# Input projections of a hybrid decoder step on one core: order of weight splits, bias table, key turns and bias strips

## The chip, the cores and the metric

The kernel runs on one core of a Trainium2 chip. The metric is the device time of one execution in microseconds (us); lower is better. Before the change the median of three runs is 2732.77 us (2732.03 to 2739.77).

## The reference

The reference is one inference step of two layers, for a prompt of 1024 tokens and 8 samples of 8 tokens each (64 rows). The change touches the first stage of layer 0:

```python
def attn_projections(xn, w_in, ...):
    h = jnp.einsum('btd,de->bte', xn, w_in)          # xn = rmsnorm(x), 1024 wide
    qa, ka, va, qi, ki, wi, hb = jnp.split(h, ...)
    q_a = rmsnorm(qa per head); k_a = rmsnorm(ka per head)
    ...                                              # three window groups: q_b, k_b normed, v_b
sc   = sum over 8 heads of wi * relu(qi . ki)        # index scores, then top 256 keys of each row
bias = rel_bias[rel_bucket(distance)]                # one table of 32 buckets x 20 heads
```

Sparse attention, window attention, the output projection, the squared-ReLU MLP and a recurrent layer with its own MLP follow in later stages.

## The kernel before, in words

The whole kernel is written by hand for five engines with semaphores. `stage_project` (line 363) is the first stage. It multiplies 9 tiles of rows (tile 0 holds the 64 sample rows, tiles 1 to 8 the prompt, 128 rows each) with 8 groups of columns, `GROUPS`: group 0 `kikv` (328 columns: index keys, index weights, keys, values), group 1 `qi` (index queries, 512), group 2 `qa`, groups 3 to 5 `qk0..2`, group 6 `v01`, all 512, and group 7 `v2` (256). Below, "(g, i)" is tile i of group g, and a step is one such pair.

A product is made in three passes of fp32r with a high and a low part of both operands: (x high, w high), (x high, w low), (x low, w high), for each of 8 slices k of the contraction, so 24 matmuls a tile (`project`, line 772; its `piece` and `pieces` cut the 24 into equal runs). Group 0's first seven tiles run slice by slice as the input arrives (line 846).

The weights of a slice k of a group, a "unit", come in by DMA from SyncE's queue (`load_w`, line 515) into one of three raw buffers. VectorE makes the high part (`split_high`, line 922), GpSimd the low part (`split_unit_low`, line 600). A raw buffer is free for the unit three later when its low part is made. A group may begin on TensorE when all 8 low parts of it are there (`w_low`).

ScalarE copies a finished tile out of PSUM into one of three row buffers (line 721, `copied`), squares the heads that have a norm (line 741), and takes the roots one step later (line 674). VectorE sums the squares (`norm_sum`), inverts the roots of the tile before and multiplies (`norm_apply`, line 975). GpSimd multiplies by the gains (line 640, `gained`), and SyncE stores the row buffer (`store`, line 533). ScalarE may overwrite a row buffer when it is stored. A tile p on TensorE needs the rows of tile p-3 copied, since there are three PSUM banks for it.

The order is an order in code on each engine, by the step (g, i):

- GpSimd: in group 0 it makes the low part of unit i+2 of group 1 (`FIRST_SPLITS` = 2), then waits for the normed tile i and multiplies by the gains. In group 1 it makes the units of group 2. From group 2 on, the units come from the list `WEIGHTS_AT`: first the units of the step, then the gains of the same step. VectorE norms tile i only in step i+1.
- VectorE: in group 0 the high part of unit i+2 of group 1, then `norm_sum` of tile i, then `norm_apply` of tile i-1. From group 2 on: high parts of the step's units, `turn` (lines 303 to 312: three tiny operations that close one bit of the search for the 256th score on four tiles), one or more bits of its own two tiles (lines 250 to 271), `norm_sum` of the step, `norm_apply` of the step before.
- ScalarE: from group 2 on also `show` (line 292), four sign passes over the score rows for the bit of the step (`SHOW_AT`: three steps in four). A bit needs the bound that VectorE's `turn` has written.
- TensorE: (0,7), (0,8), (1,0), then six matmuls that make the bias table of 20 heads and 3000 columns (line 860, into PSUM banks that group 0 used: the first waits until rows (0,6) are copied), then (1,1), then the key turns (line 871, nine transposes in three lots, each lot waits until ScalarE has taken the one before from the one bank), the sample query turns (line 800), and (1,2), (1,3), (1,4). From (1,5) on the tiles are done in four pieces between the index scores.
- SyncE: in group 1, step 0, it waits for the table in SBUF, writes it to DRAM and twice in halves, and waits for all three (`tab_out`). The key turns wait for `tab_out` too, since the buffer of the table is used again. Then come the bias strips, shifted copies from DRAM to DRAM: two DMAs of 2 MB (`bias_strips`, steps (1,0) and (1,1)) and three of 512 KB (`window_strips`, steps (1,2) to (1,4)), each ahead of the weight load and the row store of its step. The row store of a step is that of the tile two steps before.

## Time and profile before

| what | us |
|---|---|
| median of three runs | 2732.77 |
| the profiled execution | 2738.89 |
| its span | 2737.0 |
| first stage ends, by the profile | about 462 |
| TensorE busy, of the span | 2637.9 |
| waits of TensorE in the first stage on low parts of weights | 12.2 |

The profile is one execution. Times in it are counted from the start of the span. TensorE is busy 96% of the span, so a change can only bring what TensorE waits, what it runs at the lower clock, or what it does twice. The first stage is 462 us of the 2737; all later stages begin behind it in order.

### The profile page before, as it was taken

The numbers are of one execution on the slowest core, as the hardware profiler recorded it, in microseconds if no ns is written. First come the engines' busy times: TensorE is split into PE (matmuls) and PEld (weight loads), VectorE is DVE, ScalarE is ACT, GpSimd is POOL, SyncE is SP. The second block draws the span as 40 slices with busy tenths as digits, with TensorE's granted clock in tenths as the row PEclk, the third lists the DMA queues.
The fourth block names the chain that finished last, engine by engine and source line by source line (L and its number), as shares of the span: only waits on it lengthen the run. The fifth ranks groups of instructions, "written<-read, shape, count | busy, mean of one in ns | idle before, by whom it ended". The sixth has DMA issues, their size and how long they took to land.

```text
span 2737.0 us, 39752 instructions
## 1 busy us (share of the span) xinstructions
PE 2637.9 (96%) x15960; PEld 2445.8 (89%) x15960; DVE 1145.2 (42%) x1978; ACT 781.2 (29%) x1400; POOL 955.1 (35%) x470
## 2 busy tenths in 40 slices
PE   7999998988889999999999999998999999999999
PEld 6667787856569999999999999998999999999999
DVE  5369975446455222222222266655432222222222
ACT  5358884865422010001001033353211001000100
POOL 4114440036235333234234363333343234323332
PEclk9999999989889999999999999999999999999999
DMA  4402223642551111111111112142111111111112
GB/s 146 133 26 80 87 89 103 209 108 70 170 193 47 47 46 46 38 46 46 38 46 46 38 31 86 66 160 93 41 50 44 46 46 38 46 39 45 46 41 86
DMA packets 109196, 198.65 MB, mean 73 GB/s; under 512 B 22709, under 2 KB 62773, under 8 KB 108805
## 3 DMA queue, kind: packets, MB, share of 16 engines
q1 hardware_dynamic: 104602, 191.85, 22.4%
q10 hardware_dynamic: 4480, 5.27, 0.6%
q8 instruction: 72, 1.18, 0.2%
q14 instruction: 42, 0.34, 0.0%
HBM read 170.97 MB, written 47.17 MB: 80 GB/s over the span
## 4 chain that ended last, share of the span: by engine, by line
PE 64%; issue 3%; POOL 2%; DVE 1%; ACT 1%; DMA 0%; POOLq 0%; DVEq 0%; ACTq 0%
PE d_ps L2249 63%; POOL m_hidden_low L2579 2%; PE d_ps L2872 1%; ACT m_relu L2603 1%; PE d_ps L2264 1%; POOL unit_low L2236 1%; DVE unit_high L2232 0%; DVE xg_low L3000 0%; PE d_ps_sums L2307 0%; DMA mixed_low<-mixed_t 0%; DVE r_tanh L2984 0%; DVE mixed_low L2449 0%; POOLq L2525 0%; DVE r_input_gate L2978 0%; DVE r_tanh L2972 0%
## 5 line engine op out<-in xcount | busy, mean ns | idle before, releaser
L2236 POOL TENSOR_TENSOR unit_low<-unit_raw,unit_high 128x1024 fp32r<-128x1024 f32 x160 | 449.5, 2810 | 1191.8 <-DVE unit_high L2232 1191.2
L2249 PE MATMUL d_ps<-xg_high,unit_high 128*128 128x364 f32 (+1 forms) x2112 | 472.4, 332 | 5.7 <-DVE xg_low L3000 3.1
L2249 PE MATMUL d_ps<-xg_low,unit_high 128*128 128x364 f32 (+1 forms) x2112 | 464.8, 328 | 0.0
L2249 PE MATMUL d_ps<-xg_high,unit_low 128*128 128x364 f32 (+1 forms) x2112 | 464.5, 328 | 0.0
L2603 ACT ACTIVATE m_relu<-d_ps 128x1092 f32<-128x1092 f32 x64 | 69.3, 1083 | 1177.8 <-PE d_ps L2249 1177.8
L2666 DVE TENSOR_TENSOR x_t<-x_t,d_ps 128x1092 f32<-128x1092 f32 x128 | 165.3, 1292 | 520.1 <-PE d_ps L2249 520.1
L2249 PEld LDWEIGHTS d_ps<-xg_high,unit_high 128*128 128x128 f32 x2112 | 366.2, 188 | 11.4 <-DVE xg_low L3000 4.2
L2249 PEld LDWEIGHTS d_ps<-xg_high,unit_low 128*128 128x128 f32 x2112 | 366.9, 189 | 0.0
L2249 PEld LDWEIGHTS d_ps<-xg_low,unit_high 128*128 128x128 f32 x2112 | 365.3, 188 | 0.0
L2249 PE MATMUL d_ps<-m_hidden_high,unit_high 128*128 128x364 f32 (+1 forms) x1536 | 340.6, 330 | 3.9 <-POOL m_hidden_low L2579 3.9
L2249 PE MATMUL d_ps<-m_hidden_high,unit_low 128*128 128x364 f32 (+1 forms) x1536 | 338.5, 328 | 0.0
L2249 PE MATMUL d_ps<-m_hidden_low,unit_high 128*128 128x364 f32 (+1 forms) x1536 | 337.8, 328 | 0.0
L2653 DVE TENSOR_TENSOR m_relu<-m_relu,rstd_all 128x1092 f32<-128x1092 f32 x64 | 86.4, 1350 | 562.3 <-ACT m_relu L2603 562.3
L2249 PEld LDWEIGHTS d_ps<-m_hidden_high,unit_high 128*128 128x128 f32 x1536 | 264.0, 188 | 11.9 <-POOL m_hidden_low L2579 8.7
L2249 PEld LDWEIGHTS d_ps<-m_hidden_high,unit_low 128*128 128x128 f32 x1536 | 265.9, 188 | 0.0
L2249 PEld LDWEIGHTS d_ps<-m_hidden_low,unit_high 128*128 128x128 f32 x1536 | 265.6, 188 | 0.0
L785 PE MATMUL proj_ps<-w_high,x_high 128*128 128x512 f32 (+2 forms) x520 | 202.6, 390 | 13.1 <-POOL w_low L608 12.2
L785 PE MATMUL proj_ps<-w_low,x_high 128*128 128x512 f32 (+2 forms) x520 | 198.5, 382 | 0.0
L785 PE MATMUL proj_ps<-w_high,x_low 128*128 128x512 f32 (+2 forms) x520 | 198.2, 381 | 0.0
L2579 POOL TENSOR_TENSOR m_hidden_low<-m_square,m_hidden_high 128x1092 fp32r<-128x1092 f32 x64 | 164.0, 2562 | 6.4 <-DVE m_square L2658 6.4
L785 PEld LDWEIGHTS proj_ps<-w_high,x_high 128*128 128x128 f32 x520 | 99.8, 192 | 46.7 <-POOL w_low L608 13.3
L2232 DVE CAST unit_high<-unit_raw 128x1024 fp32r<-128x1024 f32 x158 | 111.8, 708 | 62.2 <-PE d_ps L2249 58.8
(370 smaller groups left out, 3102.8 us busy)
## 6 DMA issues: line engine op xcount, KB each, us to landing
unit_raw<-w_units SPq DMA_DIRECT2D x160, 512.0 KB, 3.5
unit_raw<-w_in SPq DMA_DIRECT2D x48, 256.0 KB, 2.9
proj_rows<-rows SPq DMA_DIRECT2D x32, 256.0 KB, 2.0
s_win<-win_cache SPq DMA_DIRECT2D x2, 3968.0 KB
proj_rows<-rows SPq DMA_DIRECT2D x36, 128.0 KB, 1.8
sw_rows<-proj_rows SPq DMA_DIRECT2D x12, 384.0 KB, 4.9
select_work<-xt SPq DMA_DIRECT2D x8, 546.0 KB, 3.9
x_t<-xt SPq DMA_DIRECT2D x4, 1092.0 KB, 13.0
```

The lines of the kernel that those rows point to most:

```text
L785: last = nc.tensor.matmul(ps[p % 3][:, 0:w], x[:, k, c:c + P], y[gi % 2][:, k, 0:w], start=(n == 0), stop=(n == len(passes) - 1))
L2232: self.nc.vector.tensor_copy(self.wh[slot][:, :], self.raw[:, slot, :]).then_inc(self.w_high, 1)
L2236: self.nc.gpsimd.tensor_tensor(self.wl[slot][:, :], self.raw[:, slot, :], self.wh[slot][:, :].bitcast(F32), ALU.subtract).then_inc(self.w_ ...
L2249: last = self.nc.tensor.matmul(ps[:, c, 0:USED[c]], w[wslot][:, wk], v[:, k, c, 0:USED[c]], start=(k == 0 and n == 0), stop=(k == nk - 1 a ...
L2264: last = self.nc.tensor.matmul(ps[:, c, 0:USED[c]], w[wslot][:, wk], v[:, k, c, 0:USED[c]], start=(k == 0 and n == 0), stop=(k == nk - 1 a ...
L2579: nc.gpsimd.tensor_tensor(hl[:, i, :, :], v[:, i % 2, :, :], hh[:, i, :, :].bitcast(F32), ALU.subtract).then_inc(h_low, 1)
L2603: nc.scalar.activation(r[:, i % 2, :, :], ps[slot][:, :, 0:CH], ACT.Relu).then_inc(d.taken[slot], 1)
L2653: nc.vector.tensor_tensor(r[:, i % 2, :, :], r[:, i % 2, :, :], d.rstd[:, :, :], ALU.mult).then_inc(relu_scaled, 1)
L2666: nc.vector.tensor_tensor(d.x[:, n, :, :], d.x[:, n, :, :], ps[s][:, :, 0:CH], ALU.add).then_inc(d.taken[s], 1)
L2872: last = nc.tensor.matmul(ps[use % 2][:, c, 0:CC], gw[:, n % 2, x, :], cv[:, n % 2, c, :], start=True, stop=True)
```

## The change

It changes only `stage_project`:

- Loads: six instead of three units of group 1 are loaded ahead of the loop (units 3, 4 and 5 behind the load of the table's selector); the loop then loads unit 6 at (0,1) and unit 7 at (0,2).
- Splits: three instead of two units of group 1 are split ahead of the loop; the other five follow the lists `SECOND_HIGH` on VectorE and `SECOND_LOW` on GpSimd: by (0,3) all are done.
- GpSimd's gains from group 2 on come one step later in its order: low parts of the units of step n, then the gains of step n-1.
- TensorE: the six table matmuls stand between six pieces of (1,1), four matmuls each; the three lots of key turns stand between the four pieces of (1,2), six matmuls each; the sample query turns follow (1,2).
- SyncE: the stores of (0,7) and (0,8) come first in steps (1,0) and (1,1); the wait for `tab_out` moves to (1,1); the 16 halves of the bias strips go out as eight DMAs of 512 KB, so that with the three of the window strips there are eleven, one a step from (1,1) on, each ahead of the load of its step and in group 2 ahead of the row store.

```diff
-        FIRST_LOADS = 3
-        FIRST_SPLITS = 2
+        FIRST_LOADS = 6
+        FIRST_SPLITS = 3
+        SECOND_HIGH = [(3,), (4, 5), (6,), (7,)]
+        SECOND_LOW = [(3, 4), (5,), (6,), (7,)]
...
                 sp.dma_start(pick, a["bias_pick"]).then_inc(S["pick_in"], 16)
+                for k in range(3, FIRST_LOADS):
+                    load_w(1, k)
...
-            shifts = [(strips[x:x + AH], halves, HW, x * HW, AH, SEQ // 2) for x in (0, AH)]
+            shifts = [(strips[x:x + 2], halves, HW, x * HW, 2, SEQ // 2) for x in range(0, 2 * AH, 2)]
...
+                if gi == 1 and i < 2:
+                    store(*steps[x - 2])
...
+                if gi == 1 and i == 1:
                     sp.wait_ge(S["tab_out"], 16 * 3)
-                if gi == 1 and i < len(shifts):
-                    dst, rows, pitch, off, nh, w = shifts[i]
+                if NT + 1 <= x <= NT + len(shifts):
+                    dst, rows, pitch, off, nh, w = shifts[x - NT - 1]
...
-                k = i + (FIRST_LOADS if gi == 0 else 0)
-                if gi < 2 and k < KD:
+                k = i + (FIRST_LOADS - 1 if gi == 0 else 0)
+                if gi < 2 and (gi, i) != (0, 0) and k < KD:
                     load_w(gi + 1, k)
...
-                if x >= 2 and steps[x - 2][0] != 1:
+                if x >= 2 and steps[x - 2][0] != 1 and gi != 1:
                     store(*steps[x - 2])
...
             for gi in range(NGR):
                 for i in range(NT):
-                    k = i + (FIRST_SPLITS if gi == 0 else 0)
-                    if gi < 2 and k < KD:
-                        split_unit_low(pool, gi + 1, k)
...
+                    if gi == 0:
+                        for k in SECOND_LOW[i] if i < len(SECOND_LOW) else ():
+                            split_unit_low(pool, 1, k)
+                        gain(gi, i)
+                        continue
+                    if gi == 1:
+                        for unit in [(2, i)] if i < KD else [(3, k) for k in range(AHEAD_3)]:
+                            split_unit_low(pool, *unit)
+                        continue
+                    if i < NT - 1:
                         for unit in WEIGHTS_AT[NT * (gi - 2) + i]:
                             split_unit_low(pool, *unit)
-                    for h0, hn, row, _ in kinds(gi):
...
+                    if (gi, i) != (2, 0):
+                        gain(*((gi, i - 1) if i else (gi - 1, NT - 1)))
+                    if i == NT - 1:
+                        for unit in WEIGHTS_AT[NT * (gi - 2) + i]:
+                            split_unit_low(pool, *unit)
+                if gi == NGR - 1:
+                    gain(gi, NT - 1)
...
             for c in range(NTC):
+                project(1, 1, c, NTC)
...
                 nc.tensor.matmul(table_bank(c)[0:NBH, 0:n], relb[:, :], pick[:, 512 * c:512 * c + n],
                                  start=True, stop=True).then_inc(S["tab_mm"], 1)
-            project(1, 1)
+            project(1, 2, 0, 4)
...
                 last.then_inc(S["turned"], 1)
-            for i in range(1, NT):
+                project(1, 2, t + 1, 4)
+            turn_queries(0)
+            for i in range(3, NT):
                 if i - 3 in SEL_TILES:
                     project_with_scores(1, i, i - 3, i - 2)
                     continue
-                if i > 1:
-                    project(1, i)
-                if i == 1:
-                    turn_queries(0)
+                project(1, i)
...
             for i in range(NT):
-                if i + FIRST_SPLITS < KD:
-                    split_high(1, i + FIRST_SPLITS)
+                for k in SECOND_HIGH[i] if i < len(SECOND_HIGH) else ():
+                    split_high(1, k)
                 norm_sum(0, i)
```

`gain(gi, i)` is the old loop over `kinds(gi)` (wait for `normed`, multiply by the gains) as a function.

## Rows read from the trace of the kernel before

**Rows 1.** Waits of PE, 0 to 420 us: total, times, longest us.

```profile
PE proj_ps L785 <- POOL w_low L608: 12.2, 3, 5.9
```

**Rows 2.** Timeline of PE: start us, us, line op, tiles, [idle before <- releaser].

```profile
52.23 0.80 PE L785 MATMUL proj_ps<-w_high,x_high 128*128 128x512 f32 x1 [5.86 <-POOL w_low L608]
...
60.64 5.99 PE L860 MATMUL score_ps<-select_work,bias_table 33*20 33x512 f32 x12
66.56 0.79 PE L785 MATMUL proj_ps<-w_high,x_high 128*128 128x512 f32 x1
...
74.66 0.75 PE L871 MATMUL turn_ps<-ident,kiwi_sb 64*128 64x64 f32 x4
...
78.81 0.79 PE L785 MATMUL proj_ps<-w_high,x_high 128*128 128x512 f32 x1
...
99.67 0.92 PE L818 MATMUL score_ps<-late 64*128 64x384 f32 x4 [0.69 <-ACT late L656]
```

**Rows 3.** Stretch: us; PE, PEld, DVE, ACT, POOL busy (x); PEclk, DMA share, GB/s.

```profile
52.20:57.00 4.80, 4.77 (x11) 3.81 (x12) 1.17 (x7) 1.73 (x7) 0.51 (x2) 0.50 0.23 63
74.60:78.80 4.20, 2.42 (x18) 1.50 (x17) 0.56 (x3) 1.51 (x4) 0.07 (x1) 0.97 0.62 217
81.80:97.00 15.20, 15.20 (x66) 12.10 (x65) 0.83 (x2) 1.17 (x2) 1.30 (x1) 0.99 0.60 212
```

**Rows 4.** Timelines of POOL, DVE, ACT and SP, 40 to 58 us; landing of loads.

```profile
40.20 0.47 POOL L640 TENSOR_TENSOR rows<-rows,unit_raw 128x128 f32<-128x128 f32 x1 [1.66 <-DVE rows L975]
45.63 0.58 POOL L640 TENSOR_TENSOR rows<-rows,unit_raw 128x128 f32<-128x128 f32 x1 [0.74 <-DVE rows L975]
50.91 1.26 POOL L608 TENSOR_TENSOR w_low<-unit_raw,w_high 128x512 fp32r<-128x512 f32 x1
...
41.06 1.13 DVE L928 CAST w_high<-unit_raw 128x512 fp32r<-128x512 f32 x1 [0.94 <-DMA unit_raw<-w_in]
...
43.76 0.47 ACT L721 ACTIVATE rows<-score_ps,rstd_rows 128x256 f32<-128x256 f32 x1 [2.77 <-DMA proj_rows<-rows]
55.08 0.47 ACT L721 ACTIVATE rows<-proj_ps,rstd_rows 128x256 f32<-128x256 f32 x1 [3.14 <-DMA proj_rows<-rows]
...
50.41 2.83 SPq L580 DMA_DIRECT2D sample_w_t<-kiwi_rows  x8
...
DMA to landing us min/median/max: 2.7/3.1/3.3
```

**Rows 5.** Timelines of SP and ACT, 67 to 86 us.

```profile
67.21 0.36 SPq L553 DMA_DIRECT2D bias_rows<-late  x1
71.08 0.78 SPq L560 DMA_DIRECT2D bias_strips<-bias_halves  x1
...
85.56 0.69 ACT L721 ACTIVATE rows<-proj_ps,rstd_rows 128x512 f32<-128x512 f32 x1 [7.43 <-DMA proj_rows<-rows]
```

**Rows 6.** Timelines of PE, DVE, POOL and ACT, 270 to 350 us.

```profile
280.39 0.80 PE L785 MATMUL proj_ps<-w_high,x_high 128*128 128x512 f32 x1 [5.64 <-POOL w_low L608]
332.76 0.50 PE L785 MATMUL proj_ps<-w_high,x_high 128*128 128x512 f32 x1 [0.66 <-POOL w_low L608]
...
271.17 0.42 DVE L928 CAST w_high<-unit_raw 128x512 fp32r<-128x512 f32 x1
...
279.07 1.27 POOL L608 TENSOR_TENSOR w_low<-unit_raw,w_high 128x512 fp32r<-128x512 f32 x1
...
325.03 0.67 ACT L721 ACTIVATE rows<-proj_ps,rstd_rows 128x512 f32<-128x512 f32 x1
...
349.72 0.69 ACT L721 ACTIVATE rows<-proj_ps,rstd_rows 128x512 f32<-128x512 f32 x1 [2.29 <-PE proj_ps L785]
```

**Rows 7.** One line: engine op xcount, ns min/median/max, first and last start.

```profile
L310 DVE TENSOR_SCALAR select_flip<-select_count x31: 169/170/1228, 206.9 to 427.3; 128x4 int32<-128x4 int32 x31
```

**Rows 8.** Timelines of DVE and PE at the end of the stage.

```profile
459.51 0.69 DVE L359 TENSOR_SCALAR select_work<-late 128x1024 f32<-128x1024 f32 x1
...
462.17 1.09 PE L1578 MATMUL sw_ps_x<-ident,unit_raw 128*128 128x128 f32 x4 [3.29 <-PEq L371]
```

More of the change, by code:

```diff
@@ L624, in _, with gain @@
             pool.wait_ge(S["small_in"], 48)
+            def gain(gi, i):
+                n = rows_n(gi, i)
+                for h0, hn, row, _ in kinds(gi):
+                    pool.wait_ge(S["normed"], NORM_AT[gi, i] + 1)
+                    v = st[:, n % NST, HD * h0:HD * (h0 + hn)].rearrange("p (h d) -> p h d", h=hn)
+                    nc.gpsimd.tensor_tensor(v, v, gains[:, row:row + 1, :].broadcast_to([P, hn, HD]),
+                                            ALU.mult).then_inc(S["gained"], 1)
@@ L625, in _ @@
             for gi in range(NGR):
                 for i in range(NT):
-                    k = i + (FIRST_SPLITS if gi == 0 else 0)
-                    if gi < 2 and k < KD:
-                        split_unit_low(pool, gi + 1, k)
-                    if gi == 1 and i == NT - 1:
-                        for k in range(AHEAD_3):
-                            split_unit_low(pool, 3, k)
-                    if gi >= 2 and i < NT - 1:
+                    if gi == 0:
[3 more added lines that the diff above has]
+                        continue
@@ L634, in _ @@
+                    if gi == 1:
[3 more added lines that the diff above has]
+                    if i < NT - 1:
                         for unit in WEIGHTS_AT[NT * (gi - 2) + i]:
                             split_unit_low(pool, *unit)
-                    for h0, hn, row, _ in kinds(gi):
-                        n = rows_n(gi, i)
-                        pool.wait_ge(S["normed"], NORM_AT[gi, i] + 1)
-                        v = st[:, n % NST, HD * h0:HD * (h0 + hn)].rearrange("p (h d) -> p h d", h=hn)
-                        nc.gpsimd.tensor_tensor(v, v, gains[:, row:row + 1, :].broadcast_to([P, hn, HD]),
-                                                ALU.mult).then_inc(S["gained"], 1)
@@ L642, in _ @@
-                if gi >= 2:
-                    for unit in WEIGHTS_AT[NT * (gi - 2) + NT - 1]:
-                        split_unit_low(pool, *unit)
+                    if (gi, i) != (2, 0):
[5 more added lines that the diff above has]
+                    gain(gi, NT - 1)
```

## The prediction

> **What bounds the kernel now.** The page comes first: TensorE is busy 96% of the span (the table above), so the question is where in the first stage it waits or runs slowly. The waits of TensorE name it: three waits on low parts of weights, 12.2 us, the longest 5.9 [rows 1]. TensorE's timeline shows where. One stands ahead of (1,0), 5.86 us, the other ahead of (4,0), 5.64, the third ahead of (5,0), 0.66 [rows 2, 6]. The stretches show the price of the clock: at 0.50 eleven matmuls took 4.8 us, 0.43 each; at 0.99 66 took 15.2, 0.23 each, so 5.5 for a tile of 24 [rows 3]. Tile (1,0) took 60.64 - 52.23 = 8.4 us and (1,1) 74.66 - 66.56 = 8.1: both began at 1.2 GHz, the one behind an idle engine, the other behind six table matmuls of 20 columns' output [rows 2]. From 60.64 to 99.67, 39.0 us, TensorE did four tiles (22.1), the table (5.9) and the turns; the other 8 or so are low clock and waits.
>
> **Part 1, weights of group 1 ahead of the norms.** Before, the eighth low part ends at 50.91 + 1.26 = 52.17, and (1,0) starts at 52.23 [rows 2, 4]. After, GpSimd's order is: units 3 and 4, gains of tile 0, unit 5, gains of tile 1, unit 6, gains of tile 2, unit 7. So the last unit still stands behind the gains of tile 2, and those behind the store of tile 0, since there are three row buffers. VectorE must split unit 5 ahead of the sum of tile 1, with which it norms tile 0. Unit 5's load can go when the low part of unit 2 is made, which was at 40.20 - 1.66 = 38.54 and is now some 0.7 earlier, 37.8 (my estimate: its high part no longer stands behind the first row means), and lands 3.1 later at 40.9; the split beside a GpSimd operation takes 1.13 as the one at 41.06 did, to 42.1; sum and norm 0.9 more, so the gains of tile 0 come at 43.0, not 40.20: 2.8 later. From gains 0 to the row copy of tile 3 it was 43.76 - 40.20 = 3.56, from that copy to gains 2 it was 45.63 - 43.76 = 1.87; then 0.58 and a split of 1.26 [rows 4]: 43.0 + 3.56 + 1.87 + 0.58 + 1.26 = 50.3. The part wins 1.9 us of 5.86, not all of it. Bounds: 0 (each norm later by as much as the splits are earlier) and 3.5.
>
> What is late next: (1,1) needs rows (0,7) copied. That was 55.08 + 0.47 = 55.55, behind eight small DMAs of SyncE (2.83 us) [rows 4], with 5 us to spare before the table ended. All norms of group 0 come 2.8 later, so 58.4 now. Tile (1,0) takes 8.4 at the low clock: 50.3 + 8.4 = 58.7. If the shorter idle keeps the clock up it ends at 55.9 and waits for the copy until 58.4: so 58.4 to 58.7 either way.
>
> **Part 2, table between the pieces of (1,1).** The work stays: 5.5 for the tile, 5.9 for the table, of which the last matmuls ran at half clock; I take 5.2. What may go is the low clock behind the table, 8.1 - 5.5 = 2.6 us. Each table matmul now has four wide ones beside it. Bounds: the clock stays up (10.7 us for both) or falls in the middle (the second half at half speed, 5 more). I take 10.7, because the index scores, small matmuls between pieces of a tile as well, run from 99.67 on without a wait, and the stretch up to 97 with tiles alone stands at 0.99 [rows 2, 3]. So 58.7 + 10.7 = 69.4.
>
> **Part 3, key turns between the pieces of (1,2).** The turns took 78.81 - 74.66 = 4.15 us, with PE busy 2.42 [rows 2, 3]; the 1.7 of waits for ScalarE now have pieces of 1.4 over them. But (1,1) used to cover the way of the table to DRAM: from the end of the table, 66.56, to `tab_out`, 71.08 at the latest (SyncE goes on there), is 4.5 us [rows 2, 5]. Now one piece of 1.4 covers it, and TensorE waits 3.1: **a new stall**, 70.8 to 73.9. Behind TensorE's wait stand the turns, ScalarE's copies of them, its root for (0,8), and so the store of (0,8) on SyncE, ahead of page loads and strips; nothing of these is due on TensorE before (1,4). Then three pieces (4.1) and the turns (2.4): 80.4. A low clock behind the stall costs 0 to 3; I take 1.6: 82.0.
>
> **Part 4, strips behind the stores.** The copy of rows (1,1) waited 7.43 us for a store [rows 5] that had a 2 MB strip ahead of it in the queue. Before, (1,2) to (1,4) went from 78.81 to 99.67, 20.9 for 16.6 of work: 1.6 low clock by my estimate, the rest the query turn and the waits around it. After, rows are copied in time; (1,3), (1,4) take 11.1, turn and take 1.4: 82.0 + 12.5 = 94.5 against 99.67. **Front: 5.2 us.** The eleven strip DMAs cost SyncE 0.78 each to issue [rows 5], six more than before, 5 us beside steps of 5.5 to 11 us, hidden by the units of group 2 whose loads wait for splits anyway; a 512 KB piece ahead of a load or store delays it by a quarter of what 2 MB did, and the strips are read only in the next stage. Without that cover a load is late by about 3 us, with tens of us until (2,0). I cost it at nothing.
>
> **Part 5, gains one step later on GpSimd.** The last unit of group 4 had its high part at 271.17, its low part only at 279.07, because the gains of the step before stood between; PE started at 280.39 [rows 6]. Now the low part follows at about 271.6 and ends at 272.9, before TensorE is ready at 280.39 - 5.64 = 274.75. Gains of a tile could never start before VectorE norms it in the next step, so no store is later. But the rows of p-3 limit TensorE too: for (5,0) those of (4,6), copied at 325.03 + 0.67 = 325.7. ScalarE and VectorE had no wait for TensorE here, so this time stays, and (5,0) can start at 325.75 instead of 332.76: **7.0 us**, not the 5.64 + 0.66 + 1.6 (clock) = 7.9 that were there. From 349.72 ScalarE waits for TensorE (2.29) [rows 6], so the gain lasts. At the end of the stage VectorE is done at 460.2, TensorE's next work starts at 462.17 [rows 8]; both follow from TensorE's group 6, and shift with it.
>
> **Sum.** 5.2 + 7.0 = 12.2. The profiled execution's 2738.89 (span 2737.0 and 1.9 around it) would become 2726.7. It was 6.1 above the median of the runs, 2732.77, which becomes 2720.6. About 0.3%, 8.2 us, is what a measurement of this kernel can tell from no change.
>
> **Rivals.** (A) The front gives almost nothing: the clock falls in the mixed table and stays low behind the stall. Place: 62 to 80 us. Price 5, front 0.2, time 2725.6. For it: the clock did fall during the table. Against: half of the mix is full tiles. (B) The boundary gives little, because ScalarE's and VectorE's chain is the limit from group 2 on: then 5 to 6 in all, 2727. For it: (5,0) is already limited by 325.7. Against: the row at 349.72. (C) Better: no low clock at all in the front (1.6), and bits of the search start earlier by 1 at group changes, since two splits no longer run back to back there: 2717.5. (D) Slower. `turn`'s tiny operation takes 0.170 as a median, and 1.228 where it stands beside a GpSimd operation [rows 7]. The split now may follow the high part directly, exactly where `turn` runs. If each of the 31 turns loses 1.06, and ScalarE's chain, the limit for (5,0), with it, the boundary's 7.0 are not won and 31 x 1.06 = 33 us are lost less what is lost already and what slack takes, about half: 2732.77 - 5.2 + 17 = 2744.6. It decides from 12 new collisions on. Against: a gain starts when VectorE norms, takes longer than VectorE needs to reach the next high part, and the split follows it then as before, only one unit further on. That the splits are not ahead of the norms as named is in part 1: one of eight stays behind three gains.
>
> The Trainium skill, page "SBUF — State Buffer", section "SBUF: two separate sides", says that GpSimd and some VectorE operations hold a port pair exclusively and that the second to come fully blocks. By that rule (D)'s mechanism is real, and the maximum in the row agrees; it does not say how often it happens.
>
> **How the numbers follow.** Forecast 0.60, A 0.14, B 0.10, C 0.10, D 0.06. Faster by over 0.3% (below 2724.6) is the forecast and C, with a little of A: 0.72. Within 0.3%: most of A and B: 0.22. Slower: D, 0.06. The range 2714 to 2730 takes in C with the runs' own spread and A and B with theirs; D and part of the tails are left out.
>
> **What would show it.** In the new profile: first matmul of (1,0) at about 50.3 after 3.9 us idle; the table's matmuls spread over some 10 us from 58.7 at a granted clock of 1.00; a wait of about 3 us ahead of the first key turn, put down to SyncE or a DMA; first index scores near 94.5; no wait on `w_low` at (4,0) and (5,0), a short one on ScalarE's rows at (5,0) instead; the stage's end near 450. Wrong would make it: (1,0) still at 52, a clock of 0.5 through 60 to 80, long waits on `rows` between 200 and 340, or the median of line 310 near 1.2 us.

## The result, and the profile after

The changed kernel is **slower**. Of five runs four took 2758.71 to 2775.6 us; the fifth took 4234.95, with TensorE's clock granted at 0.56 of full speed over the whole kernel, and is left out of the ratio. The median of all five is 2772.31. Five runs of the kernel before on the same occasion gave a median of 2739.77. The ratio is 1.0115, 95% interval 1.0096 to 1.0133, so some 32 us more. I had forecast 2720.6, within 2714 to 2730, and given "slower" 0.06.

| | before | after |
|---|---|---|
| profiled execution, us | 2738.89 | 2758.71 |
| span, us | 2737.0 | 2756.8 |
| PE at the index scores (front) | 99.67 | 94.09 |
| PE at the end of the stage | 462.17 | 491.30 |

The two last rows split the result. The front did what was forecast: the scores begin 5.6 us earlier. Between them and the end of the stage 29.1 + 5.6 = 34.7 us are lost. (What follows the stage is the same code. It took 2737.0 - 462.17 = 2274.8 in the one execution and 2265.5 in the other, and 2265.5 to 2279.0 over all profiled ones; so spans are a blunt measure here, and the end of the stage is the better one.)

The waits of PE in the kernel after, from 0 to 480 us (total, times, longest us), answer to [rows 1]:

```profile
PE score_ps L834 <- ACT late L682: 23.0, 5, 10.3
PE proj_ps L801 <- POOL w_low L615: 5.5, 3, 3.0
```

The waits on low parts fell from 12.2 us to 5.5, but a new one of 23.0 stands on top: the index scores wait for ScalarE's relu (line 682). The timeline of PE after, against [rows 2, 6, 8]:

```profile
48.52 0.50 PE L801 MATMUL proj_ps<-w_high,x_high 128*128 128x512 f32 x1 [3.04 <-POOL w_low L615]
56.84 0.47 PE L801 MATMUL proj_ps<-w_high,x_high 128*128 128x512 f32 x1 [0.94 <-ACT rows L737]
...
73.93 1.16 PE L888 MATMUL turn_ps<-ident,kiwi_sb 64*128 64x64 f32 x4 [3.04 <-DMA bias_halves<-late]
94.09 0.92 PE L834 MATMUL score_ps<-late 64*128 64x384 f32 x4 [0.83 <-ACT late L672]
121.66 3.65 PE L834 MATMUL score_ps<-late 64*128 64x512 f32 x4 [10.26 <-ACT late L682]
144.01 4.21 PE L834 MATMUL score_ps<-late 64*128 64x512 f32 x8 [6.80 <-ACT late L682]
166.36 4.77 PE L834 MATMUL score_ps<-late 64*128 64x512 f32 x8 [5.12 <-ACT late L682]
...
491.30 1.09 PE L1594 MATMUL sw_ps_x<-ident,unit_raw 128*128 128x128 f32 x4 [3.29 <-PEq L371]
```

Up to 94.09 this is the forecast's list (50.3, 58.4 to 58.7, 69.4, 73.9, 94.5). Then three waits of 5 to 10 us, 22 us apart. They are 22.2 of the 34.7 us. The rest is mostly the clock, which is low in a stretch at or behind each wait. Columns: stretch; its length, PE, PEld, DVE, ACT and POOL busy (x); granted clock, DMA share, GB/s. First three stretches of the kernel after, then the first of them in e10_rows4, a version below that has no such wait:

```profile
115.50:129.20 13.70, 7.54 (x16) 3.86 (x18) 5.39 (x7) 2.99 (x5) 1.44 (x1) 0.52 0.21 72
142.80:153.00 10.20, 8.99 (x22) 4.94 (x24) 5.50 (x6) 3.31 (x5) 1.39 (x1) 0.53 0.24 79
166.70:177.00 10.30, 10.30 (x27) 4.93 (x26) 4.63 (x5) 3.03 (x4) 0.00 (x0) 0.53 0.44 145
```

```profile
115.50:129.20 13.70, 13.70 (x70) 8.35 (x68) 11.46 (x22) 7.29 (x11) 3.67 (x2) 1.00 0.43 147
```

TensorE is busy for 26.8 us in the three stretches at about half the clock, so some 13 us are lost there (an estimate: half of 26.8).

What releases the waits is read backwards through the timelines of ACT and DVE of the kernel after:

```profile
120.91 0.60 ACT L682 ACTIVATE late<-score_ps 128x512 f32<-128x512 f32 x1 [12.65 <-DVE select_work L953]
...
120.00 0.43 DVE L944 CAST w_high<-unit_raw 128x512 fp32r<-128x512 f32 x1 [10.66 <-DMA unit_raw<-w_in]
```

ScalarE waited 12.65 us for VectorE to free a score buffer (line 953), and VectorE had stood 10.66 us at a weight split (line 944) whose unit had not landed (16.21 at an earlier one, at 97.81). The unit is one of group 2, which TensorE begins only at 180.34, 60 us later; but the split stands in VectorE's order between two additions of scores, and so a late load that nobody needs yet stops the scores. The loads themselves, line 523 from 80 to 180 us (ns min/median/max; first and last start; who waited; landing us):

```profile
L523 SPq DMA_DIRECT2D unit_raw<-w_in x10: 594/7260/9997, 84.9 to 166.8; - x10
  DVE w_high L944: 45.7, 5
DMA to landing us min/median/max: 9.7/16.5/19.2
```

Before, a load landed 3.1 us after issue in the front [rows 4], with no strip ahead of it. Here the median is 16.5, and SyncE needs 7.26 us for the issue alone. That is no new kind of delay. In the kernel before the three loads issued from 70 to 100 us, beside its large strips, had it as well, and VectorE waited 10.96 us for one of them (line 519 there is line 523 here):

```profile
L519 SPq DMA_DIRECT2D unit_raw<-w_in x3: 3862/5478/7519, 71.9 to 91.8; - x3
DMA to landing us min/median/max: 11.4/13.2/16.4
```

What was there behind two strips is now there behind eight. SyncE's timeline shows what stands ahead of each load:

```profile
91.78 0.70 SPq L567 DMA_DIRECT2D bias_strips<-bias_halves  x1
92.54 7.06 SPq L523 DMA_DIRECT2D unit_raw<-w_in  x1
...
102.36 0.69 SPq L567 DMA_DIRECT2D bias_strips<-bias_halves  x1
103.11 7.90 SPq L523 DMA_DIRECT2D unit_raw<-w_in  x1
```

The next strip goes at 113.78, so from here on there is one each 10.6 to 11.4 us. And what the DMA engines did from 97 to 100 us, behind one such strip (the packets and their mean rate, then the queue's packets, MB and share of 16 engines' time):

```profile
DMA packets 92, 0.15 MB, mean 51 GB/s; under 512 B 6, under 2 KB 22, under 8 KB 92
q1 hardware_dynamic: 92, 0.15, 13.3%
```

The piece of 512 KB takes 0.524 MB / 51 GB/s = 10.3 us (an estimate from the rate), about as long as 2 MB at 200. Eight pieces are 82 us of queue: the first is issued at 84.08, the last at 155.4.

The reading that this suggests: a DMA runs on so many engines as its outermost count has, and `strips[x:x + 2]` has two. The Trainium skill, page "DMA: Bandwidth & Descriptors", section "Why a DMA increments its semaphore by 16 and not by 1", states such a rule: the largest number up to 16 that divides the slowest dimension of both access patterns. The 13.3% agree with 2 of 16. The experiments had to show whether this, and not the number of DMAs, their new place or the other parts, makes the loss.

### The profile page after: what moved, and what is told of

It reads as the page before. It is cut to its first block, busy times and chain, and to the rows that moved or that the text cites. A ratio compares the mean times of both kernels' runs of the same rounds, so it can differ in the third digit from the quotient of the medians.

```text
span 2756.8 us, 39758 instructions
## 1 busy us (share of the span) xinstructions
PE 2641.0 (96%) x15960; PEld 2443.1 (89%) x15960; DVE 1149.7 (42%) x1978; ACT 782.1 (28%) x1400; POOL 953.8 (35%) x470
## 4 chain that ended last, share of the span: by engine, by line
PE 64%; issue 3%; POOL 2%; DVE 1%; ACT 1%; DMA 0%; ACTq 0%; POOLq 0%; DVEq 0%
PE d_ps L2265 62%; POOL m_hidden_low L2595 1%; PE d_ps L2888 1%; ACT m_relu L2619 1%; POOL unit_low L2252 1%; DVE unit_high L2248 0%; DMA mixed_low<-mixed_t 0%; DVE xg_low L3016 0%; PE d_ps_sums L2323 0%; PE d_ps L2280 0%; ACTq L2416 0%; DVE r_tanh L3000 0%; POOLq L2541 0%; DVE r_input_gate L2994 0%; DVE x_t L2682 0%
## 5 line engine op out<-in xcount | busy, mean ns | idle before, releaser
L2619 ACT ACTIVATE m_relu<-d_ps 128x1092 f32<-128x1092 f32 x64 | 69.2, 1082 | 1177.8 <-PE d_ps L2265 1177.8
L615 POOL TENSOR_TENSOR w_low<-unit_raw,w_high 128x512 fp32r<-128x512 f32 (+2 forms) x64 | 83.6, 1311 | 164.5 <-DVE w_high L944 164.5
```

What stands on the lines that cost most here:

```text
L615: nc.gpsimd.tensor_tensor(wl[gi % 2][:, k, 0:w], wraw[:, u % NRAW, 0:w], wh[gi % 2][:, k, 0:w].bitcast(F32), ALU.subtract).then_inc(S["w_l ...
L2619: nc.scalar.activation(r[:, i % 2, :, :], ps[slot][:, :, 0:CH], ACT.Relu).then_inc(d.taken[slot], 1)
```

## The experiments

Ratios are to runs of the kernel before that were made on the same occasion; they compare the runs of both as a whole and are not the quotients of the medians. Medians of different lines can come from different occasions, so small differences are better read from the ratios. Every edit is against the changed kernel, unless another is named.

| run | what differs | median us | ratio, 95% |
|---|---|---|---|
| after | | 2772.31 | 1.0115 (1.0096, 1.0133) |
| e1_rows16 | after, strips of 16 rows by 16 partitions | 2735.73 | 0.9988 (0.9977, 0.9999) |
| e9_rows8 | after, 8 rows by 32 | 2728.86 | 0.9977 (0.9964, 0.9991) |
| e10_rows4 | after, 4 rows by 64 | 2727.53 | 0.9972 (0.9960, 0.9985) |
| e2_two_strips | after, two strips of 2 MB | 2742.70 | 1.0027 (1.0008, 1.0047) |
| e3_eight_alone | before + strips of 2 rows | 2765.97 | 1.0101 (1.0080, 1.0123) |
| e8_rows16_alone | before + strips of 16 rows | 2734.86 | 0.9993 (0.9983, 1.0003) |
| e4_gains_alone | before + GpSimd's order | 2731.48 | 0.9982 (0.9970, 0.9994) |
| e6_mix_alone | before + mixed table | 2744.50 | 1.0029 (1.0017, 1.0041) |
| e5_no_mix | e1 without the mixed table | 2726.20 | 0.9957 (0.9944, 0.9969) |
| e7_low7 | e5, last two low parts adjacent | 2721.38 | 0.9953 (0.9938, 0.9967) |
| e11_cover | e1, more tile ahead of the turns | 2722.62 | 0.9957 (0.9937, 0.9977) |

**The shape of the strips.** The same bytes, the same number of DMAs, the same places; only the outermost count is 16 instead of 2.

```
-shifts = [(strips[x:x + 2], halves, HW, x * HW, 2, SEQ // 2) for x in range(0, 2 * AH, 2)]
+shifts = [(strips[x:x + 16, y:y + 16], halves, HW, x * HW - y, 16, SEQ // 2)
+          for x in range(0, 2 * AH, 16) for y in range(0, P, 16)]
-    ap=[[pitch, nh], [-1, P], [1, w]]
+    ap=[[pitch, nh], [-1, dst.shape[1]], [1, w]]
```

> The changed kernel with the bias strips in eight pieces of the same 512 KB at the same places, but each piece holds 16 of the 128 shifted rows of all 16 half heads instead of all 128 rows of two. Theory F (few engines: a strip DMA whose slowest dimension is 2 runs on two of the 16 DMA engines, at 50 GB/s, so that the weight loads of group 2 queue behind it): pieces at 200 GB/s or more, loads of group 2 land in under 6 us instead of 16.5, VectorE's 45.7 us of waits for them go, no wait over 1 us of the index scores between 100 and 180 us, median 2718 to 2726. Theory P (place and number: a strip, two pages and a load a step, one behind the other on SyncE's queue, hold the loads whatever the pieces look like): loads still 10 us or more, median above 2750.

2735.73 us, 36.6 less than the changed kernel. The loads, again line 523 from 80 to 180 us:

```profile
L523 SPq DMA_DIRECT2D unit_raw<-w_in x12: 328/349/602, 80.6 to 166.2; - x12
  DVE w_high L944: 6.9, 1
DMA to landing us min/median/max: 2.5/3.0/3.8
```

From 7260 ns to 349 for an issue, from 16.5 us to 3.0 for a landing, from 45.7 us of VectorE's waits to 6.9; the scores' waits are gone. Both shapes copy 256 runs of 2 KB in a DMA, so the length of a run is not what differs. The loss is the shape of the strips. The time is above the 2718 to 2726 of theory F, though: only 0.1% of gain is left, not the 0.4% forecast; that is taken up below.

**Two large strips in the new place.** This undoes the cut and leaves the place behind the stores.

```
-shifts = [(strips[x:x + 2], halves, HW, x * HW, 2, SEQ // 2) for x in range(0, 2 * AH, 2)]
+shifts = [(strips[x:x + AH], halves, HW, x * HW, AH, SEQ // 2) for x in (0, AH)]
```

> The changed kernel with the 16 half heads as two DMAs of eight (2 MB) again, at steps (1,1) and (1,2), all else as changed. Theory F: they run on eight engines at 200 GB/s and are out of the way in some 25 us, waits of the index scores 0 to 5 us, median 2720 to 2732. Theory P: fewer DMAs, but the same five places as before the change one step later: 2725 to 2740 also. If it stays above 2755, the loss does not come from the cut of the strips but from the order of TensorE or GpSimd.

2742.7 us. Each strip has 8 rows, as in [rows 3]; at the 25.5 GB/s of an engine above it takes 10.3 us. Loads landed at 4.1 us as a median, 16.8 as a maximum, VectorE waited 23.3 us in 3 times, and one score wait of 3.79 us is left, at 116.28. So two strips block the queue too, but for 20 us and not for 82. The time is above what either theory gave (2720 to 2732, 2725 to 2740), and the stage ends at 464.32: two large strips in the new place cost the whole gain of the rest.

**The shape alone.** Two kernels made from the one before: only the eight pieces (and the places one step later), once of two rows, once of sixteen.

```
+shifts = [(strips[x:x + 2], halves, HW, x * HW, 2, SEQ // 2) for x in range(0, 2 * AH, 2)]
-if gi == 1 and i < len(shifts):
-    dst, rows, pitch, off, nh, w = shifts[i]
+if NT <= x < NT + len(shifts):
+    dst, rows, pitch, off, nh, w = shifts[x - NT]
```

> The kernel before with only the strips cut in eight pieces of two half heads, one a step from (1,0) on. Theory F and theory P both: the index scores wait for VectorE's weight splits as in the changed kernel, 20 to 35 us, so 2755 to 2775, and row stores of (0,7), (0,8) still behind the first pieces. If it is within 8 us of the kernel before, the loss needs the rest of the change too.

> The kernel before with only the strips in eight pieces of 16 shifted rows, one a step from (1,0) on: the counterpart of e3, same places, same bytes. Theory F: the 28 us of e3 are gone, and the row stores land in 3 us, so that the 1.1 + 0.7 us ahead of the first scores go: 0.9985 to 1.000. Theory P: within 8 us of e3, near 1.010.

2765.97 and 2734.86 us: 31 us between them, and both within what theory F gave. The timeline of PE in the one of two rows has the same three waits as the changed kernel, though no other part of the change is in it (the second and third are 6.80 us at 143.50 and 5.03 at 165.75; the first is):

```profile
121.13 3.65 PE L818 MATMUL score_ps<-late 64*128 64x512 f32 x4 [5.71 <-ACT late L666]
```

**The dose.** Four and eight rows in the same places, to see whether the loss follows the engines step by step.

```
+strips[x:x + 8, y:y + 32] ... 8 ...  for x in range(0, 2 * AH, 8) for y in range(0, P, 32)
+strips[x:x + 4, y:y + 64] ... 4 ...  for x in range(0, 2 * AH, 4) for y in range(0, P, 64)
```

> Strips in the same eleven places and of the same 512 KB, but each of the eight cut as 8 rows of strips by 32 partitions. Theory (a DMA runs on as many engines as divide its outermost count, and what its neighbours lose is the time it lies on them): the one of 16 rows took few us and loads landed at a median of 3.0; two rows gave 10 us and 16.5. With 8 rows: some 200 GB/s, loads landing at a median of 3 to 5, the largest 5 to 8, DVE's wait for a load about 7 to 10 us, no score waits of 5 us or more from 100 to 180, and 2730 to 2745 us. Rival (it is the number of rows that one descriptor spans, or the place, not the engines): landing 10 or more again and 2755 or more.

> The same with 4 rows by 64 partitions. Theory: 4 engines, about 100 GB/s, 5 us for a strip; loads behind one land up to 5 us later, 8 at a median, against 16.5 with two rows; next to no wait of TensorE, since units have some 11 us: 2735 to 2750 us. Rival: a loss in proportion to the time of a strip, half of the 28 to 30 us of two rows, which gives 2750 to 2757.

2728.86 us and 2727.53. Line 523 from 80 to 180 us, first with eight rows (VectorE waited 8.5 us once), then with four:

```profile
L523 SPq DMA_DIRECT2D unit_raw<-w_in x13: 323/339/1443, 85.8 to 174.9; - x13
DMA to landing us min/median/max: 2.6/5.2/8.1
```

```profile
L523 SPq DMA_DIRECT2D unit_raw<-w_in x13: 322/1121/4262, 85.5 to 174.9; - x13
  DVE w_high L944: 12.4, 3
DMA to landing us min/median/max: 2.6/9.4/13.3
```

The landing goes 16.5, 9.4, 5.2, 3.0 us for 2, 4, 8 and 16 rows: that follows the engines. The time does not: 2772, 2728, 2729, 2736. Four rows cost nothing that can be told from eight, less even than the text expected (2735 to 2750), and the rival of a loss in proportion (2750 to 2757) falls. Eight rows are the fair pair to the two strips of 2 MB, which have eight rows as well: with the same bytes at the same rate in pieces of 512 KB the stage ends at 453.77 instead of 464.32. So the cut itself was right, and only its direction wrong. Why there is a threshold can be read from SyncE's strips. With four rows the eight go out from 84.7 to 120.7 us (line 567): 36.0 us, 5.1 from one to the next. That is the pace of the work and not of the strips, since with eight rows it is the same (84.9 to 120.8). What the DMA engines did with four rows, from 95 to 97 us:

```profile
DMA packets 102, 0.21 MB, mean 103 GB/s; under 512 B 1, under 2 KB 2, under 8 KB 102
q1 hardware_dynamic: 102, 0.21, 26.4%
```

That is twice the rate and twice the share of two rows. At 103 GB/s a strip takes 5.1 us, so the queue ends each step about where it began it. On two engines it takes 10.3, the queue falls behind by 5 with every strip, and the last one went at 155.4 instead of 120.7, 34.7 us late. (That the stage lost 34.7 between 94.09 and its end as well is chance to the tenth: its parts are the 22.2 us of waits and the low clock.) A load that lands 13.3 us after its issue did no harm there; what did was a queue that falls further behind with each step.

**GpSimd's order alone.** The kernel before with only the new order of gains and low parts from group 2 on.

```
+if (gi, i) != (2, 0):
+    gain(*((gi, i - 1) if i else (gi - 1, NT - 1)))
+if i == NT - 1:
+    for unit in WEIGHTS_AT[NT * (gi - 2) + i]:
+        split_unit_low(pool, *unit)
```

> The kernel before with only GpSimd's order from group 2 on changed (split of the step's units, then the gains of the step before). My step of the sum: no wait on low parts at (4,0) and (5,0), a short one on ScalarE's rows instead, 7.0 us less: ratio about 0.9974, 2725 to 2729 where the kernel before gives 2732. Rival D (more collisions of the turn operations): slower by 10 or more. Rival B (ScalarE and VectorE are the bound): 0 to 2 us less.

2731.48 us; by the ratio 4.9 less than before (interval 1.6 to 8.2), where 7.0 was forecast. The profiled execution is the slowest of twelve (2743.92): its clock stood at 0.50 from 179 to 191 us, where that of the kernel before was 1.00, and its stage ends at 463.06, no earlier than before. To read the order without this and without the front, take two executions that differ in it and have the same tile's wait for rows as a mark behind that stretch. From e8_rows16_alone (GpSimd's old order), then from e4_gains_alone, both PE:

```profile
257.12 0.50 PE L785 MATMUL proj_ps<-w_high,x_high 128*128 128x512 f32 x1 [0.43 <-ACT rows L721]
279.74 0.80 PE L785 MATMUL proj_ps<-w_high,x_high 128*128 128x512 f32 x1 [5.65 <-POOL w_low L608]
461.77 0.63 PE L1578 MATMUL sw_ps_x<-ident,unit_raw 128*128 128x128 f32 x4 [3.29 <-PEq L371]
```

```profile
262.67 0.50 PE L794 MATMUL proj_ps<-w_high,x_high 128*128 128x512 f32 x1 [0.42 <-ACT rows L730]
332.34 0.51 PE L794 MATMUL proj_ps<-w_high,x_high 128*128 128x512 f32 x1 [1.42 <-POOL w_low L608]
383.76 0.50 PE L794 MATMUL proj_ps<-w_high,x_high 128*128 128x512 f32 x1 [1.05 <-POOL w_low L608]
463.06 0.63 PE L1587 MATMUL sw_ps_x<-ident,unit_raw 128*128 128x128 f32 x4 [3.28 <-PEq L371]
```

461.77 - 257.12 = 204.65 against 463.06 - 262.67 = 200.39: 4.3 us. The wait of 5.65 at (4,0) is gone, but (5,0) waits 1.42 on a low part and (6,0) 1.05.

**The mixed table alone, and the change without it.** The pieces of (1,1) between the table's matmuls, put into the kernel before; and e1_rows16 with the table in one run.

```
 for c in range(NTC):
+    project(1, 1, c, NTC)
...
-project(1, 1)
```

> The kernel before with only the six pieces of (1,1) between the table matmuls; the key turns follow at once and wait for the table's way to DRAM (4.5 us) with nothing over it. If the clock holds: 10.7 us for table and tile instead of 14, then 4.5 of stall and a clock that is low once behind it: 0 to 3 us slower than before. Theory C: in some executions slower by 8 or more, ratio 1.001 to 1.004, and a low clock of 10 us or longer inside 60 to 100 us of the profile if it falls there.

> The kernel of e1 (strips in pieces of 16 shifted rows) with the six table matmuls in one run again and (1,1) in one piece behind them, ahead of the first piece of (1,2); the key turns stay between the pieces of (1,2). Theory C (clock: in the mix of table and tile matmuls TensorE's clock falls in some executions and stays low until the first scores, as it did for 27 us in the profile of e1 but not in the changed kernel's): scores start near 92, the low clock at 50 to 90 us is at most 14 us long, and the median is 6 to 9 us below that of e1, ratio about 0.995 to 0.997. Theory S (the new stall of 3 us ahead of the key turns is what eats the front's gain, the clock is chance): also better, but by 3 us or less, ratio 0.998. Theory N (the front gives nothing because what follows is bound by VectorE's and ScalarE's chain): same as e1, 0.9988.

2744.5 us (slower by 0.29%) and 2726.2 (9.5 less than e1_rows16). Both ratios are what theory C gave, that the clock falls in the mix. The windows say otherwise. The columns are as above. First the changed kernel in the mixed table and behind the stall, then e6_mix_alone behind its stall (its mix, 60.60 to 71.00, stands at 1.00 too), then e5_no_mix, the end of the table and the tile behind it:

```profile
58.90:69.90 11.00, 11.00 (x34) 4.53 (x34) 0.34 (x2) 3.50 (x7) 0.46 (x1) 1.00 0.09 31
74.20:80.80 6.60, 6.60 (x27) 5.15 (x26) 0.75 (x3) 2.09 (x5) 0.26 (x1) 0.76 0.00 0
```

```profile
76.69:86.00 9.31, 7.52 (x26) 5.40 (x27) 1.09 (x5) 1.51 (x4) 0.45 (x1) 0.50 0.52 181
```

```profile
58.90:70.00 11.10, 11.10 (x27) 6.66 (x28) 0.27 (x1) 3.04 (x6) 0.46 (x1) 0.60 0.30 79
```

In the mix the clock is 1.00 in both kernels; it falls behind the stall that the mix uncovers, to 0.76 on average and to 0.50 (1.2 GHz). Where the table runs in one piece the mean from its end into the tile behind it is 0.60. What is bad in e6_mix_alone is the wait for the table's way to DRAM, which has no tile over it there, and the clock behind it; its scores start at 105.71, 6.0 us later than before:

```profile
76.69 1.17 PE L871 MATMUL turn_ps<-ident,kiwi_sb 64*128 64x64 f32 x4 [4.55 <-DMA bias_halves<-late]
```

One execution was different: in e1_rows16 the clock was at 0.50 through the mix and the stall, from 58.5 to 85.8, 27.3 us in which about 13 were lost against the full clock (an estimate: half of the busy time). Its scores start at 102.79, 8.7 us later than in the changed kernel, which begins (1,1) at the same time.

```profile
58.50:85.80 27.30, 25.51 (x48) 10.89 (x47) 0.72 (x4) 4.57 (x8) 0.51 (x2) 0.50 0.13 33
```

Of the seven executions profiled with a mixed table (after, e1, e2, e6, e9, e10, e11) it is the only one. Nor does the clock fall behind the stall each time. In e2_two_strips, with a stall of 3.06 us, it does not:

```profile
74.65:80.00 5.35, 5.35 (x27) 4.14 (x27) 0.78 (x3) 2.09 (x5) 0.29 (x1) 1.00 0.02 7
```

**The stall covered.** To separate mix and stall: e1_rows16 with three of the four pieces of (1,2) ahead of the key turns instead of one.

```
-project(1, 2, 0, 4)
+for t in range(3):
+    project(1, 2, t, 4)
...
-    project(1, 2, t + 1, 4)
+    if t == 0:
+        project(1, 2, 3, 4)
```

> Strips of 16 rows as in e1_rows16; three pieces of (1,2) ahead of the key turns and one between them, where one was ahead and three between. The table stays mixed with (1,1). Theory (the 3 us stall ahead of the turns is only uncovered work, the low clock comes from the mix of table and tile): no wait of 1 us or more on the bias halves ahead of the first turn, scores 3 us earlier than in e1_rows16 in an execution of the same clock, 2731 to 2736 us. Rival (the stall also brings the clock down, so most of what e5_no_mix won was the stall): 2727 or less, and clock 1.00 behind the turns. Other rival (ScalarE's copies between turns, no longer covered, cost 1.7 again): 2734 to 2738, waits of 0.5 to 0.9 us ahead of the second and third turn.

2722.62 us, 13 less than e1_rows16 in medians and 8.5 by the ratios, and as good as e5_no_mix with its table in one run. PE's timeline, and the windows of the mixed table and of the turns:

```profile
74.44 0.72 PE L889 MATMUL turn_ps<-ident,kiwi_sb 64*128 64x64 f32 x4 [0.23 <-DMA bias_halves<-late]
...
91.66 0.92 PE L834 MATMUL score_ps<-late 64*128 64x384 f32 x4 [0.83 <-ACT late L672]
```

```profile
58.00:74.40 16.40, 16.20 (x53) 7.49 (x51) 1.34 (x7) 4.96 (x11) 0.91 (x2) 1.00 0.20 50
74.44:79.00 4.56, 3.42 (x24) 2.54 (x24) 0.48 (x3) 2.09 (x5) 0.00 (x0) 1.00 0.04 17
```

The stall is 0.23, ScalarE's copies cost 0.69 again (and 0.46 ahead of the sample's query turn), the clock is 1.00 in both stretches, and the scores start at 91.66, where e9_rows8 and e10_rows4, equal but for the stall (and the strips' shape), had 94.94 and 94.72. So 3.1 to 3.3 us, against 3.04 of stall, 1.15 given back for the copies, and a clock of 0.68 and 0.50 behind the stall in those two. Against e2_two_strips, with the stall but no low clock, it is 93.26 - 91.66 = 1.6. So about half of the gain is the stall itself and half the clock behind it. Of the texts the rival has it: 2727 or less and a clock of 1.00 behind the turns, where the theory gave 2731 to 2736. With the stall covered, the mixed table costs nothing that these runs can tell.

The end of the stage doesn't show this gain: 455.00 in e11_cover, 453.77 and 453.71 in e9_rows8 and e10_rows4. What can account for it stands further on, at 171 to 184 us in e11_cover:

```profile
171.00:184.00 13.00, 13.00 (x45) 9.56 (x44) 3.86 (x14) 3.95 (x8) 2.02 (x7) 0.51 0.32 81
```

In e10_rows4 the clock is 1.00 there, through the same code. At half the clock 13.0 us lose some 6.5 (an estimate), which is more than the 4.4 by which e11_cover falls behind from the scores to the end. The same fall stands in e4_gains_alone (179 to 191) and in e1_rows16 (182 to 196). What brings it about is open.

**The last low part.** e5_no_mix with `SECOND_LOW = [(3, 4), (5,), (6, 7)]`, so that no gain stands between the last two low parts.

> The kernel of e5 with the low part of unit 7 of group 1 ahead of the gains of tile 2 on GpSimd. My step 1 (the last unit stands behind the gains of tile 2): (1,0) starts 1 to 2 us earlier, and since the table's first matmul needs rows (0,6) and not (0,7), the gain is kept: 1 to 2 us below e5. If the load of unit 7 or VectorE's order is the bound: the same as e5.

2721.38 us; by the ratios not to be told from e5_no_mix. Tile (1,0) started 0.94 earlier (47.78 against 48.72), but the table then waited 2.95 us for ScalarE, against 0.34 in e5_no_mix, and the scores started at 91.21 against 90.48. The next wait stood right behind the one removed.

The best versions, e5_no_mix, e7_low7 and e11_cover, beat both kernels, by 0.4 to 0.5% the one before. Their intervals overlap, and which is best stays open.

## Why the prediction was wrong, point by point

**The step that failed is in part 4:** "a 512 KB piece ahead of a load or store delays it by a quarter of what 2 MB did". It took the rate as a property of the queue. The rate belongs to the DMA: 51 GB/s for two rows, some 200 for eight. A quarter of the bytes took the same 10 us. From there the next sentence fell too ("Without that cover a load is late by about 3 us"): loads landed 13 us later than in the front before, as late as behind the 2 MB strips, and "tens of us until (2,0)" looked at the wrong reader. TensorE needed the unit late; VectorE's split of it stands in the middle of the scores. "I cost it at nothing" stands against 22.2 us of waits of the scores and some 13 of low clock behind them. The rival that I missed had its place (84 to 166 us), its price (eight pieces x (10.3 - 5.1) = 42 us of queue, of which 35 came through) and its point of decision (a strip longer than the step it stands in). The 10.3 could have been worked out from the diff's `2` and [rows 3], where strips of eight rows stand with 212 GB/s and 0.60 of 16 engines; the step of 5.1 us was measured only afterwards, the prediction had 5.5 to 11.

**Part 1** was right in its main point and 1.8 us off. (1,0) started at 48.52, not 50.3, after a wait of 3.04 (forecast 3.9): the last unit does stand behind three gains. The gains of tile 0 came at 42.10, not 43.0, and from there to the last split (47.20) it was 5.1 us, not 6.0. (1,1) was then held by rows (0,7), as forecast, 0.94 us, from 56.84 (forecast 58.4).

**Part 2** had the clock right, 1.00 in the mix, and the duration short: from 56.84 to the first matmul of (1,2) at 69.23 are 12.4 us, not 10.7. With part 1's error this gave 69.2 against 69.4, two errors that cancel: that (1,2) began on time is luck. Rival A (clock low in mix and stall) came true in one of seven executions, not in the changed kernel's.

**Part 3** was right: the new stall is 3.04 us (3.1) and ends at 73.93 (73.9), and the clock behind it fell, to 0.76. I priced the stall rightly and did not see that it was worth removing: with three pieces over it, the scores start 3 us earlier, about half of it by the clock.

**Part 5** was right in mechanism and too large: 7.0 forecast, 4.3 in the timelines and 4.9 by the ratio measured. The term mis-sized is what is late next: I had ScalarE's rows alone limit (5,0). Low parts still come 1.42 late at (5,0) and 1.05 at (6,0). From the mark (257.78 in the kernel before) to (5,0) the forecast has 68.0 us, and e4_gains_alone has 332.34 - 262.67 = 69.7; these 1.7 and the 1.05 at (6,0) are the missing 2.7. Of the 1.7 some 0.7 are ScalarE's: rows (4,6) are copied 67.9 us behind the mark before (325.70) and 68.6 now (331.31). The other 1.0 is the low part: VectorE's high part of the last unit ended at 330.46, but GpSimd was at the gains of the tile before (329.37 to 331.02) and ended the low part at 332.29: one gain still stands ahead of the last split.

**Rival D** did not come true. Line 310, the tiny operation of the search, in e8_rows16_alone and then in e4_gains_alone (from 200 to 470 us: sum in us, mean ns; idle before):

```profile
L310 DVE TENSOR_SCALAR select_flip<-select_count 128x4 int32<-128x4 int32 x31 | 16.8, 542 | 1.1
```

```profile
L310 DVE TENSOR_SCALAR select_flip<-select_count 128x4 int32<-128x4 int32 x31 | 24.1, 776 | 1.1
```

The new order of GpSimd turns the median from 170 ns to 1212, but the sum grows by 7.3 us only. Of the 31 turns 11 took over 0.6 us before, and 18 do now: seven new ones, where the rival wanted 12 to decide. The median jumps because it stands at the sixteenth. The kernel with the new order is faster by 4.9 us all the same. What the seven cost is not shown; the 0.7 us by which ScalarE's rows (4,6) come later may be theirs. I had named the median of this line as a sign that would make the forecast wrong; a sum or a count would have been the sign.

**Sum.** With strips of eight or four rows the change is worth 0.23 to 0.28% by the ratios (e9, e10), about 6 to 8 us, and 462.17 - 453.7 = 8.4 in the end of the stage, where 12.2 were forecast. Of that gap of 3.8 us, 2.7 are part 5's; the front of e9_rows8 gave 99.67 - 94.94 = 4.7, not 5.2; 0.6 is left over. Why e1_rows16 has 2735.73 and e9_rows8 2728.86, with intervals that overlap, is open; the low clock of the one profiled execution, the slowest of its twelve (2744.33), would explain it, if it comes more often there.

The chance of 0.06 for slower was too small for a change in the shape of DMAs of which the trace of before had no row. I had bounded that cost from one side only.

## What to carry to other kernels

Before a DMA is cut into pieces, look at the outermost count of the piece: cut along an inner dimension, so that it stays as large as it was. Here a quarter of the bytes on a quarter of the engines took as long as the whole, and the queue then carried four times the time. Pieces of 5.1 us, one each 5.1 us, cost nothing that the runs can tell; pieces of 10.3 us cost some 31. And for each load that gets late, ask not when its data is needed but which instruction waits for it and what stands behind that one on its engine.

Where small work is mixed with large to cover waits, count what the large work covered at its old place; here it was a way to DRAM, a stall of 3 us was left of it, and moving two pieces of a tile ahead of it won the start of the scores 3 us. And to a wait of several us on TensorE add the clock behind it: here it was some 13 us on 22.

## What was unexpected of the hardware

- The clock through the same code is not the same in each execution: 1.00 in six, 0.50 in one, for the same mixed matmuls. A single execution's clock is no evidence for an order of instructions; the unchanged code behind the stage took 2265.5 to 2279.0 us, at mean clocks of 0.99 and 0.98.
- A VectorE operation of 4 columns takes seven times as long beside one of GpSimd: at 318.50 us in e4_gains_alone it took 1.29 us, beside a low part that ran from 318.48 for 1.30, against 0.17 alone. With 18 such turns in place of 11 the kernel was still faster.
